# Loading pages of the key and value cache as 64 rows of 4 KB, two tokens to a partition, in place of 128 rows of 2 KB

## What is computed

```python
PAST_LEN, PAGE_SIZE, MOBA_BLOCK, MOBA_TOPK = 2048, 128, 256, 3      # H_A, DH_A = 8, 64
# cache_k, cache_v (N_POOL, PAGE_SIZE, H_A, DH_A); page_table (8, 16)
kb_past = cache_k[page_table].reshape(DB, nb_full, MOBA_BLOCK, H, D)
k_mean = jnp.mean(kb_past, axis=2)                    # one mean key per block of two pages
idx, valid = _moba_select(q, k_mean, nb_full)         # 3 of 8 blocks for each query and head
s = einsum(q, keys of the chosen blocks) * scale      # and the 8 new tokens, causally
out = softmax(s) @ values
```

## Time and profile before

| | us |
|---|---|
| three runs | 1118.14, 1119.84, 1120.73 |
| their median | 1119.84 |
| the profiled execution, its own time | 1118.83 |
| its span in the profile | 1117.2 |

### The profile page before, as it was taken

One profiled execution on the slowest core, in us unless ns is written; L12 is line 12 of the kernel. 1 busy time (PEld: TensorE's weight loads), 2 busy tenths in 40 slices (PEclk: granted clock), 3 DMA queues, 4 the chain that ended last, 5 costly groups with the idle time before them and its releaser, 6 DMA issues.

```text
span 1117.2 us, 20695 instructions
## 1 busy us (share of the span) xinstructions
PE 1066.3 (95%) x7593; PEld 910.2 (81%) x7593; DVE 563.8 (50%) x1227; ACT 449.5 (40%) x1023; POOL 126.6 (11%) x227
## 2 busy tenths in 40 slices
PE   4999999999999999999988998999999999999997
PEld 4977877887777777767768886998899899889985
DVE  5254534545675655655644747443344334433456
ACT  5253233324554555555543355342144113322441
POOL 4003110221001033323331100100000000000000
PEclk8999999999999999999999999999999999999999
DMA  6432216234136799989974440223222222222222
GB/s 214 117 86 57 67 48 142 57 85 124 48 96 188 202 326 309 322 308 339 321 218 132 150 134 29 95 76 94 84 77 86 85 76 86 80 81 85 77 85 85
DMA packets 93716, 150.02 MB, mean 134 GB/s; under 512 B 9377, under 2 KB 39590, under 8 KB 93622
## 3 DMA queue, kind: packets, MB, share of 16 engines
q1 hardware_dynamic: 75040, 103.83, 30.6%
q0 software_dynamic: 11968, 39.85, 10.6%
q10 hardware_dynamic: 6614, 5.06, 1.6%
HBM read 141.62 MB, written 7.10 MB: 133 GB/s over the span
## 4 chain that ended last, share of the span: by engine, by line
PE 78%; DVE 9%; issue 4%; ACT 3%; DMA 3%; SPq 1%; POOLq 1%; ACTq 1%; POOL 0%; DVEq 0%
PE ps L462 27%; PE ps L497 19%; PE ps L890 7%; PE ps L470 4%; PE ps L1919 4%; PE ps L906 3%; PE ps L435 2%; DMA kring<-in_cache_k_dram 2%; PE ps L1928 1%; PE ps L1960 1%; DVE xn L552 1%; PE ps L1054 1%; PE ps L1074 1%; PE ps L1064 1%; ACT sP L2036 1%
## 5 line engine op out<-in xcount | busy, mean ns | idle before, releaser
L347 DVE TENSOR_TENSOR w<-w,w 128x512 fp32r<-128x512 f32 (+1 forms) x240 | 168.0, 706 | 305.6 <-ACT w L336 301.0
L336 ACT ACTIVATE w<-w 128x512 fp32r<-128x512 f32 (+1 forms) x240 | 145.2, 613 | 337.7 <-PE ps L470 172.4
L497 PE MATMUL ps<-h2T,w 128*128 128x288 f32 x1536 | 210.0, 297 | 4.3 <-DVE wide L2529 1.7
L497 PEld LDWEIGHTS ps<-h2T,w 128*128 128x128 f32 x1536 | 207.1, 189 | 7.2 <-DVE wide L2529 2.4
L462 PE MATMUL ps<-w,hid 128*128 128x512 f32 x672 | 161.6, 389 | 0.0
L462 PEld LDWEIGHTS ps<-w,hid 128*128 128x128 f32 x672 | 125.9, 188 | 26.0
L462 PE MATMUL ps<-w,hT 128*128 128x512 f32 x576 | 145.3, 401 | 1.4 <-ACT ri L811 1.4
L462 PEld LDWEIGHTS ps<-w,hT 128*128 128x128 f32 x576 | 106.0, 190 | 26.6 <-issue 4.9
L890 PE MATMUL ps<-hT,w 128*128 128x288 f32 x768 | 124.2, 305 | 0.0
L890 PEld LDWEIGHTS ps<-hT,w 128*128 128x128 f32 x768 | 104.7, 188 | 11.3 <-issue 10.6
L1886 POOL DMA_DIRECT2D vring<-in_cache_v_dram x128 | 68.8, 538 | 180.1 <-issue 180.1
(11 more groups left out here) (354 smaller groups left out, 1279.1 us busy)
## 6 DMA issues: line engine op xcount, KB each, us to landing
kring<-in_cache_k_dram SPq DMA_DIRECT2D x128, 256.0 KB, 4.1
vring<-in_cache_v_dram POOLq DMA_DIRECT2D x128, 256.0 KB, 4.5
w<-in_w_in_dram SPq DMA_DIRECT2D x88, 256.0 KB, 2.9
w<-in_w_up_dram SPq DMA_DIRECT2D x64, 256.0 KB, 2.8
w<-in_w_down_dram SPq DMA_DIRECT2D x64, 256.0 KB, 2.8
w<-in_w_out_dram SPq DMA_DIRECT2D x16, 256.0 KB, 3.0
x<-in_x_prompt_dram SPq DMA_DIRECT2D x4, 512.0 KB, 6.9
out_dram<-sC ACTq DMA_DIRECT2D x1, 2048.0 KB
```

What stands on the lines that cost most here:

```text
L336: eng.activation(spread(w_hi, n, j, width), together(w32, n, j, width), ACT.Copy)\
L347: eng.tensor_tensor(spread(w_lo, n, j, width), together(w32, n, j, width), spread(w_hi, n, j, width).bitcast(F32), ALU.subtract).then_inc( ...
L497: mm = eng.matmul(ps[:, b, 0:HALFT], w[a][:, j, i * P:(i + 1) * P], right[c][:, k, h * HALFT:(h + 1) * HALFT], start=(k == 0 and (c, a) == ...
```

## The change

A page is read as 64 rows of 4 KB, each with two tokens that lie side by side in the pool. In the ring, two neighbouring slots are seen as one of 4 KB (`two`). Page j of a group goes to partitions 0 to 63 when j is even and to 64 to 127 when it is odd, in the slot pair 2 (g % 2) + j // 2. So the two pages of a block fill one pair of slots: partition p holds tokens 2p and 2p + 1 of the first page, partition 64 + p those of the second. The number of DMAs, their 256 KB, their queues, their semaphores and all instructions of the other engines stay as they are.

```diff
     def pages(eng, pool, ring, arrived, b, g):
 
-        flat = pool.rearrange("n p h d -> n p (h d)")
+        flat = pool.rearrange("n (p two) h d -> n p (two h d)", two=2)
+        two = ring[:, :, :].rearrange("p (a two) c -> p a (two c)", two=2)
         for j in range(4):
             page = eng.value_load(pt_sb[0:1, bass.ds(b * NPAGE + g * 4 + j, 1)],
                                   min_val=0, max_val=pool.shape[0] - 1)
-            eng.dma_start(ring[:, 4 * (g % 2) + j, :], flat[bass.ds(page, 1), :, :].rearrange("a p n -> (a p) n"))\
+            eng.dma_start(two[64 * (j % 2):64 * (j % 2) + 64, 2 * (g % 2) + j // 2, :],
+                          flat[bass.ds(page, 1), :, :].rearrange("a p n -> (a p) n"))\
                .then_inc(sem(f"{arrived}{g % 2}"), 16)
```

## The result

| | before | changed |
|---|---|---|
| median of four runs, us | 1118.99 | 1199.49 (1192.8 to 1205.29) |
| profiled execution, its own time | 1118.83 | 1202.15 |
| span in its profile | 1117.2 | 1200.6 |

The changed kernel is slower by 7.1%: ratio 1.0711, 95% interval 1.0675 to 1.0747. The forecast was 1203 us.

The account below looks back on a forecast made before the run. TensorE was taken to set the pace with DMA right behind; +78 us in the middle stretch, +4 ahead and +2 behind, +84 us on 1118.83, gave 1203 us. The forecast's range was 1165 to 1242 us, chance 0.58.

Parts of the forecast that it names:

- TensorE sets the pace and DMA is right behind it: Middle stretch before the change: TensorE busy 162.37 of 168 us, DMA share 0.94, so only 6% of DMA reserve.
- 214 GB/s from the one load of the same form: Page rate taken from a traced x load, 64 rows of 4 KB onto partitions 0 to 63; 128-partition rows went at 399.
- the sum's 54 MB in 246 us: Middle stretch: 50.1 MB of pages at 214 GB/s, 234 us, plus 3.9 MB of weights at 333 GB/s, 12 us.
- The middle stretch's +78 us: From 390 to 558 us, keys and values both streaming: 246 us forecast for 168 us before.
- Rival 1: Slower, but engines fall out of step and halves partly overlap: 279 GB/s mean, +24 and +2 us, 1145 us; chance 0.20.
- A price per queue: Each queue's bytes priced at its own rate: SP's queue 333 GB/s, GpSimd's 355 GB/s.
- 5 us less for rows of 4 KB, at most: SP's queue: 25.2 MB of keys at 355 GB/s instead of 333 take 71 us of DMA time, not 76.
- +4 ahead and +2 behind: Before the middle stretch (345 to 390 us), +4 us from value pages ahead of awaited keys; after it (558 to 600), +2 us.
- Everything from 620 us on is only shifted: The rest of the kernel after the page loads: begins later but takes no longer, 0 us added.
- Rival 2, faster: The halves cost nothing in the middle stretch: above 320 GB/s there, about 1114 us, 1108 at best; chance 0.13.
- rows 8: Trace rows of the x load of 64 rows of 4 KB onto partitions 0 to 63: 214 GB/s, q1 99.0% busy.

Follow-up runs that it names:

- e_full_4k: Kernel before, but each group is two 512 KB loads of neighbouring pool pages onto all 128 partitions in 4 KB rows, page table ignored: 1109.38 us, ratio 0.9919.
- the runs with one queue: Changed kernel with only keys, or only values, loaded as 64 rows of 4 KB, the other as before: 1181.96 us (1.0574) and 1186.07 us (1.0611).
- e_half_2k: Kernel before, but each page goes to 64 partitions of one half, two rows of 2 KB on each: 1197.42 us, ratio 1.0698.
- e_low_low: Changed kernel with a group's pages issued in the order 0, 2, 1, 3, two loads low and then two high: 1214.05 us, ratio 1.0842.
- e_tail: Kernel before, but SP issues two of the four value pages in the last six groups: 1116.0 us, ratio 0.9963.
- e_step2: Changed kernel, but a block's first page goes to the even partitions and its second to the odd ones: 1124.7 us, ratio 1.0061.

## Why the prediction was right, point by point

- *TensorE sets the pace and DMA is right behind it.* Right. With DMA time a little lower (`e_full_4k`) the slots shrank by 4 us only, and with it higher all of it showed.
- *214 GB/s from the one load of the same form.* The step that carries the forecast, and right in kind: the engines are full, and each byte takes longer. In size it was a little off: the sum's 54 MB in 246 us are 220 GB/s over the stretch, and 231 were measured. The middle stretch's +78 us measured +67.4. Alternating halves do better than halves in pairs (217); that they overlap a little is the likely reason, not a shown one. Rival 1 had that mechanism, but its 279 GB/s is far off. The Trainium skill (SBUF — State Buffer, "Can I just issue two DMAs to hit both halves?") puts the gain of two halves in flight at 6%; 231 over 214 is 8%, so the trace agrees with it.
- *A price per queue* (333 GB/s for weights and all that isn't halved). It fell in the runs with one queue: unchanged loads went at 244 and 230 GB/s. In the forecast it mattered little: at 231 GB/s the 3.9 MB of weights take 17 us and not 12.
- *5 us less for rows of 4 KB, at most.* Nowhere shown clear of noise: 2 us over 128 partitions, about 0.5% on even and odd ones, nothing on halves.
- *+4 ahead and +2 behind* measured +6.6 and +3.1, the first by the later keys that it named.
- *Everything from 620 us on is only shifted.* Wrong, by +6.3 us. This made up for most of the 10.6 us that the middle was priced too high, so the total's nearness (1203 for 1199.49) is partly luck. Three places hold it. The first matmuls after the last values, 30 of L906, took 5.54 us for 4.18, at a lower clock. Ahead of the first matmuls of L435, TensorE stood idle for 2.72 us:

```profile
739.15 15.42 PE L435 MATMUL ps<-wo_res,uT 128*128 128x512 f32 x60 [2.72 <-DVE wide L2360]
```

  In the kernel before it did not stand idle there:

```profile
657.59 13.77 PE L435 MATMUL ps<-wo_res,uT 128*128 128x512 f32 x60
```

  These 60 matmuls then took 15.42 us for 13.77, again at a lower clock at first (0.79 from 739 to 747 us). The chain of waits leads from that idle time back to two weight loads that landed late:

```profile
725.36 6.54 DMA w<-in_w_out_dram
...
733.44 3.50 DMA w<-in_w_out_dram
```

  The same distance, from last values to the end, is 519.7 us in `e_half_2k`, 523.0 in `e_low_low`, 518.2 and 518.4 with one queue, 519.7 in `e_tail`. The lower clock after the last values is thus not the change's alone: in `e_tail`, without a load onto one half, the same 30 matmuls took 5.18 us. The late weight loads hold up the changed kernel and `e_low_low` by 2.7 and 2.6 us, `e_step2` by 0.6 us, and the kernel before not at all. Whether the change brings them on or they fall so in single executions was not tried, and stays open.
- *Rival 2, faster,* needed 320 GB/s in the middle. Its first argument, that rows 8 were slow because the load stood alone, is refuted by `e_step2` against the change, and its second, that alternating halves undo it, by the 231 GB/s.

## What to carry to other kernels

Ask of a load which partitions it lands on before asking how long its rows are: 64 partitions in one half cost 80 us here, the same rows on every second partition 6. Look in a trace for a load of the new form, however small, and compare its rate with a neighbour's at the same busy share; one such load priced this change to within its bounds. Don't price two queues apart: halves on one of them alone brought 63 or 68 of the 80 us.

## What the runs showed of the hardware that wasn't expected

- Loads onto 128 partitions fell from 355 to 244 GB/s (and from 333 to 230) only because the other queue's loads went to one half at a time. These two rates are worked out from the shares by queue.
- The order of four loads changed the rate from 231 to 217 GB/s.
- TensorE's granted clock was 1.00 in the middle stretch before and 0.88 in the changed kernel's. It has two levels, 2.4 and 1.2 GHz, and long waits for keys were followed by the lower one. TensorE's timeline of the changed kernel shows the same eight turns without a wait and after one of 5.28 us:

```profile
589.20 1.03 PE L1923 MATMUL ps<-ident,kring 128*128 128x128 f32 x8
...
598.51 1.97 PE L1923 MATMUL ps<-ident,kring 128*128 128x128 f32 x8 [5.28 <-DMA kring<-in_cache_k_dram]
```

  The clock in the two stretches is 1.00 and 0.50 of full speed (columns of the earlier trace rows):

```profile
588.00:590.00 2.00, 2.00 (x20) 1.99 (x17) 1.92 (x3) 0.98 (x3) 0.09 (x1) 1.00 1.06 188
598.00:600.00 2.00, 1.49 (x7) 1.49 (x8) 0.00 (x0) 0.34 (x1) 0.00 (x0) 0.50 1.04 231
```

  In the middle that is mostly hidden, as the pages set the pace. After the last values it cost the 1.4 us above, and at L435 another 1.65 us.
